# Weight buffers moved by 64 bytes, gated and summed tokens to multiples of 128 bytes

## What is computed

```python
mod = silu(c) @ w_ada + b_ada
sh1, sc1, g1, sh2, sc2, g2, sh3, sc3, g3 = split(mod, 9)
h = modulate(rms_norm(x, ffn1_norm), sh1, sc1)
x = x + 0.5 * g1 * ((silu(h @ w1) * (h @ w3)) @ w2)
h = modulate(rms_norm(x, mix_norm), sh2, sc2)
z = h @ w_in                       # 28 tiles of 128 columns
x = x + g2 * (concat(hgrn2(z), rglru(z)) @ w_out)
h = modulate(rms_norm(x, ffn2_norm), sh3, sc3)
x = x + 0.5 * g3 * ((silu(h @ w1b) * (h @ w3b)) @ w2b)
return rms_norm(x, final_norm)
```

## The kernel before

| tile | used as | before | after |
|---|---|---|---|
| `hhi`, `hlo`, `yhi`, `ylo` | tokens | 0 | 0 |
| `ghi2`, `glo2` (gated tokens) | tokens | 64 | 0 |
| `forms` (summed tokens) | tokens | 64 | 0 |
| `whi`, `wlo` (and `raw`) | weights | 0 | 64 |
| `hix`, `lox` (weight sums) | weights | 64 | 64 |
| `whi2`, `wlo2` (units 2 and 3) | weights | 64 | 0 |

## Time and profile before

### The profile page before, as it was taken

How to read it: one execution, slowest core, us unless ns; L and a number is a source line. 1 busy time by engine, 2 the same in 40 slices (tenths; PEclk the granted TensorE clock), 3 DMA queues, 4 the chain that set the end, 5 groups by cost and what they waited for, 6 DMA issues and landing times.

```text
span 1018.0 us, 18544 instructions
## 1 busy us (share of the span) xinstructions
PE 996.2 (98%) x6942; PEld 867.3 (85%) x6942; DVE 747.5 (73%) x1039; ACT 506.2 (50%) x690; POOL 227.3 (22%) x191
## 2 busy tenths in 40 slices
PE   8999999999999999999999989999999999999997
PEld 6779999999888888786677767878999999988887
DVE  6778778777787868779899995566778777683334
ACT  5545444455332134578977973465444444433221
POOL 0024453543112301100100000202444544200100
PEclk9999999999999999999999999999999999999999
DMA  9557667674788836421121202235676676552322
GB/s 353 211 171 205 167 201 182 180 211 149 254 284 288 309 103 234 154 83 62 63 84 43 83 23 81 86 119 142 167 214 185 177 213 166 186 180 89 104 83 84
DMA packets 63190, 162.21 MB, mean 159 GB/s; under 512 B 5440, under 2 KB 7760, under 8 KB 63008
## 3 DMA queue, kind: packets, MB, share of 16 engines
q1 hardware_dynamic: 44720, 110.79, 30.4%
q0 software_dynamic: 18416, 50.68, 20.3%
HBM read 159.36 MB, written 2.10 MB: 159 GB/s over the span
## 4 chain that ended last, share of the span: by engine, by line
PE 90%; DVE 4%; ACT 3%; issue 2%; DMA 1%; SPq 0%; DVEq 0%; ACTq 0%
PE psum L1889 15%; PE psum L1891 15%; PE psum L1890 15%; PE psum L1961 12%; PE psum L1963 12%; PE psum L1962 12%; PE psum L2219 1%; PE psum L2256 1%; PE psum L2262 1%; PE psum L2190 1%; PE psum L2107 1%; PE psum L2192 1%; PE psum L2191 1%; PE psum L2276 1%; DVE wlo L1107 1%
## 5 line engine op out<-in xcount | busy, mean ns | idle before, releaser
L586 ACT ACTIVATE whi<-raw 128x1024 fp32r<-128x1024 f32 x92 | 97.2, 1057 | 227.7 <-PE psum L1891 211.0
L1107 DVE TENSOR_TENSOR wlo<-raw,whi 128x1024 fp32r<-128x1024 f32 x94 | 117.7, 1253 | 120.9 <-ACT whi L586 120.6
L1891 PE MATMUL psum<-ghi,wlo 128*128 128x512 f32 (+2 forms) x384 | 143.7, 374 | 0.0
L1890 PE MATMUL psum<-glo,whi 128*128 128x512 f32 (+2 forms) x384 | 143.4, 373 | 0.0
L1889 PE MATMUL psum<-ghi,whi 128*128 128x512 f32 (+2 forms) x384 | 143.0, 373 | 0.0
L1889 PE MATMUL psum<-hhi,whi 128*128 128x512 f32 x320 | 130.8, 409 | 2.0 <-DVE wlo L1107 1.3
L1891 PE MATMUL psum<-hhi,wlo 128*128 128x512 f32 x320 | 125.0, 391 | 0.0
L1890 PE MATMUL psum<-hlo,whi 128*128 128x512 f32 x320 | 124.9, 390 | 0.0
L1961 PE MATMUL psum<-forms,whi 128*128 128x256 f32 x432 | 121.1, 280 | 0.0
L1962 PE MATMUL psum<-forms,whi 128*128 128x256 f32 x432 | 120.5, 279 | 0.0
L1963 PE MATMUL psum<-forms,wlo 128*128 128x256 f32 x432 | 120.5, 279 | 0.0
(11 more groups left out here) (270 smaller groups left out, 2349.4 us busy)
## 6 DMA issues: line engine op xcount, KB each, us to landing
raw<-wu SPq DMA_DIRECT2D x96, 512.0 KB, 3.4
ada<-wada POOLq DMA_DIRECT2D x56, 512.0 KB, 5.1
sraw_a<-ws SPq DMA_DIRECT2D x36, 512.0 KB, 6.1
raw<-ws SPq DMA_DIRECT2D x36, 512.0 KB, 6.1
sraw_b<-ws SPq DMA_DIRECT2D x36, 256.0 KB, 3.9
sraw_a<-ws POOLq DMA_DIRECT2D x18, 512.0 KB, 6.0
raw<-ws POOLq DMA_DIRECT2D x18, 512.0 KB, 5.9
early<-wada SPq DMA_DIRECT2D x16, 512.0 KB, 15.3
```

Of the source, the lines that this page charges most:

```text
L586: nc.scalar.activation(whi[:, slot, :], raw[:, slot, :], ACT.Copy).then_inc(hi_done, 1)
L1107: nc.vector.tensor_tensor(wlo[:, slot, :], raw[:, slot, :], whi[:, slot, :], ALU.subtract).then_inc(lo_done, 1)
L1890: nc.tensor.matmul(dst, a, rlo, start=False, stop=False)
L1891: return nc.tensor.matmul(dst, b, rhi, start=False, stop=stop)
```

## The change

A constant `HALF_LINE` of 64 bytes is added at three places: ahead of `raw`, `whi` and `wlo` (which moves all that follows), ahead of `hix`, and ahead of `g2`, whose address `glo2` and, by fixed distances, `h32`, `t32`, `sq0`, `whi2`, `wlo2` and `csr0` share. No instruction, wait or order is changed.

```diff
+HALF_LINE = 64
...
         hlo = sb("hlo", [P, KD, T], F32R)
+        place[0] += HALF_LINE
         raw = sb("raw", [P, 2, UNIT])
...
-        hix, off = at("hix", [P, 3, T], F32R, off)
+        hix, off = at("hix", [P, 3, T], F32R, off + HALF_LINE)
         lox, off = at("lox", [P, 3, T], F32R, off)
...
-        g2_at = off
+        g2_at = off + HALF_LINE
```

## The result

The changed kernel takes 1026.06 us in the median (1025.79 to 1027.58, 4 runs) against 1021.4 us before on the same chip: the ratio is 1.0056, with an interval of 1.0042 to 1.0070. It is slower, where 1018.7 us and faster had been forecast. The profiled execution has a span of 1024.6 us against 1018.0 before, 6.6 us more.

A forecast was written before the change was run, and what follows sets the result against it. The prediction took PE's three-fold matmuls as the bound, their pitch set by operand places modulo 128 bytes. Its terms, -12.6 + 4.1 + 3.9 + 2.0 + 0.2 = -2.4 us, gave 1018.7 us; own range 1015 to 1022, wider range 1004 to 1026.

The forecast's parts named there:

- What bounds the kernel: Whole kernel: 81% of 1018.0 us lies on six lines of three-fold matmuls, so it gains or loses nearly what they do.
- With all 84 at 113.3 ns it takes 9.52: Group stages: a group of 84 matmuls falls from 9.854 to 9.53 us with joints, 11.7 us less over 36 groups.
- T0/W64: Tokens at 0, weights at 64 modulo 128 bytes, the change's aim: 113.3 ns at 256 columns, 233.3 at 512.
- Down projections at 512 columns: Two down-projection stages: 960 matmuls rise from 229.0 to 233.3 ns, +4.1 us.
- 256-column halves: Ends of the down projections: 192 matmuls fall from 117.8 to 113.3 ns, 0.9 us less.
- Products with `hhi` and `yhi`: Other 512-column products: 588 in long stretches at +6.6 ns, +3.9 us; 468 in the mixer at +4.3 ns, +2.0 us.
- units 2 and 3 of the opening: Opening stage, weights from `whi2` and `wlo2`: 48 matmuls fall to about 226.7 ns while 48 others worsen, net nothing.
- Value units: 96 matmuls with tokens stationary and weights moving: 229.0 against 226.7 ns, +0.2 us, bounds -1.3 and +0.6.
- A: Fast rival: 512 columns at T0/W64 also save 6.7 ns, 220.0 ns; 29.3 us less, 991.8 us; chance 0.13.
- B: Middle rival: all 512-column matmuls go at 226.7 ns; 14.8 us less, 1006.3 us; chance 0.12.
- C: Slower rival: split-weight supply holds groups at 9.854 us while 512 columns pay; +9.3 us, 1030.4 us; chance 0.10.
- D: No-change rival: pitches follow tiles and their traffic, not bytes modulo 128; 1021.1 us; chance 0.05.

The follow-up runs named there:

- m1_places: TensorE alone, none of the layer: every pair of token and weight places in 64-byte steps; 226.6 to 233.3 ns at 512 columns, 113.3 to 120.0 at 256.
- m3_widths: TensorE alone: seven widths at four distances, 16 steps of 64 bytes at 256 columns, bf16 at six distances; the steps gave 113.3 or 117.8 ns.
- m2_groups: TensorE alone: a group's seven products in order for 32 sets of places; before's set 9.853 us a group, after's 9.89, best 9.520.
- k_w192_f128_x64: Kernel before with weights and gated tokens at 192 modulo 256, `forms` 128, `hix` 64; 1015.0 us, ratio 0.9946.
- k_hix192: Changed kernel with `hix`, `lox` and the gated tokens' second half 128 bytes further, `hix` at 192 modulo 256; 1026.38 us, ratio 1.0041.
- k_w_back: Changed kernel with the weights back at 128 modulo 256, all else where the change put it; 1024.18 us, ratio 1.0021.
- k_g128: Kernel before with only the gated tokens moved, to 128 modulo 256, the weights' place; 1019.11 us, ratio 0.9984.
- k_f64_x192: Kernel before with gated tokens at 128 modulo 256 like the weights, `forms` at 64, `hix` at 192; 1015.53 us, ratio 0.9938.
- k_mixer_at_192: k_w192_f128_x64 with the mixer's and output projection's tokens 64 bytes on, at 192 modulo 256 like the weights; 1013.28 us, ratio 0.9926.

## Why the prediction was wrong

*What bounds the kernel* held: 6.6 us came from the lengths of matmuls alone, and PE stayed busy in all of the group stage. The pitches read from before were read right too; every one came back on TensorE alone.

*The step that failed* is "With all 84 at 113.3 ns it takes 9.52". It took one product's pitch, `hhi` with `hix`, for the pitch of T0/W64. That product's distance is 64, modulo 256; after the change the four pairs have the distances 64 (`hhi`, `whi`), 192 (`forms`, `whi`), 64 (`forms`, `hix`) and 192 (`hhi`, `hix`). That alone doesn't decide: at both distances m1_places and m3_widths show 113.3 and 117.8 ns. What decides where the step is 64 bytes is how the pair was entered: from equal places, one step down of either operand gives the fast one, one step up the slow one (16 of 16). The kernel before follows it. From `hhi` with `whi` (both at 128) tokens step up to `forms` (192): 117.8. From `forms` with `hix` (both at 192) tokens step down to `hhi` (128): 113.3. The change made the places differ in every pair of the groups and so took away the pairs at 120.0 ns from which the fast pitch had been entered in each group. After it the steps between products are of 128 bytes. No rule was found for these, and equal places aren't a condition: m1_places, m2_groups and the first group after the change each show 113 to 114 ns without them. What the runs do show is that this set doesn't keep the fast pitch. It was lost at the next step of the tokens by 128 bytes in the first group (114.2, then 117.9 ns) and in m2_groups (113.3, then 117.8), and 117.8 stayed. Worth 13.3 us: 11.7 forecast gained, 1.6 lost.

The prediction's last sentence had said where it could break: bytes modulo 256, `forms` at 0 and `whi` at 192, 1296 matmuls at 117.8, 1024.5 us. They did stay at 117.8; the other 432 of `hhi` with `whi`, 432 of `forms` with `hix` and 864 of `hhi` with `hix` weren't at 113.3 either, but for `forms` with `hix` in the first group of each stage.

*Down projections at 512 columns*, +4.1 us forecast, were oversized: the totals of the 960 matmuls (starts less than 1 us apart) are 220.0 and 221.2 us. `ghi` with `whi` stays at distance 192 (0 and 192 after the change, 192 and 128 before) and keeps its 228.9 ns; only the products with `glo2`, at 128, are at distance 64. Two thirds at 228.9 and one at 233.3 is 230.4 ns, the pitch measured. The 256-column halves stayed at 117.8 instead of falling (0 for -0.9).

*Products with `hhi` and `yhi`*: 233.3 ns in long stretches was right, and units 2 and 3 of the opening fell to 226.7 as forecast. Their totals rose by 232.7 - 228.6 = 4.1 and 46.5 - 45.6 = 0.9 us, where 5.9 was forecast. *Value units*: 228.3 to 229.4 ns, 96 of them, +0.1 for +0.2. These matmuls' sums are +6.3 us, the stages outside the groups show +5.0: some 1.3 us went into time between other matmuls and idle time of PE, half in the opening and half in the mixer, which the prediction, counting the mixer in full, had left out. Here 1.2 + 0 + 5.0 + 0.1 - 1.3 = 5.0.

*Rivals.* A and B asked for 220 and 226.7 ns at T0/W64 and 512 columns; 233.3 came. C named the supply of split weights as a bound on the period. The stages did keep their time and 512 columns did pay, as C has it, but not for its reason: PE waited for no `wlo` there, and k_w192_f128_x64 was supplied at 9.52 us a group. D, that places do nothing, fell with m1_places. The rule cited there, the Trainium skill, "TensorE: Matmul & The Clock Gate", Part 2, of two independent read ports between which no bandwidth is taken, doesn't give the pitch for 4-byte operands: m1_places shows 226.7 against 233.3 ns with every other engine at rest, where by the rule, as the prediction used it, 16 pairs would have shown one pitch. For bf16 the measurements agree with it (215.8 ns at six distances).

*The range* ended at 1026, just short of the median. The case that came, a placement class that the trace of before doesn't hold, had been given no chance of its own: it stood in the last paragraph alone, with a number and without a weight. The pairs that the change makes could have been written down modulo 256 from the offsets; three of the four had no row.

*Settled and not.* That distance modulo 256 sets the pitch at 512 columns, and distance with what ran before that at 256, is shown with one part moved at a time. How a step of 128 bytes chooses between the two pitches is open, so a set of places has to be measured in its order of products. Why places act so isn't shown. Nor is the cause of the waits for `wlo` of 0.6 to 3 us between 115 and 138 us, which five of the eight other layer kernels' profiled executions have (k_hix192, k_w_back, k_g128, k_f64_x192, k_mixer_at_192) and those of before and after don't: in k_g128 they go back to a late DMA, with a group's places unchanged. With what follows them they add up to some 5 us, 0.5%, to one execution, so single edits were judged by pitches and stages, and only sums of several by their time.

## What to carry to other kernels

An address change must be priced by the relation of the two operands that one instruction reads, pair by pair, before and after, in the coarsest period that the trace doesn't exclude; one pair's speed isn't a property of its class. Where a pitch is bistable (two steady values at the same addresses), a stretch at the short pitch may owe it to what ran before it: removing a neighbour at the long pitch can remove the short one too. With fp32r operands, weights and tokens at equal places modulo 256 bytes for most products of 512 columns, and a set of places for 256 columns that was measured on a small loop of the real order of products, were worth 0.7% here.

## What the runs showed of the hardware

- Two fp32r operands of a matmul with a weight load before each: 226.7, 233.3, 232.0 to 233.3 and 228.9 ns at 512 columns for distances 0, 64, 128 and 192 bytes, whatever the absolute place (16 pairs, m1_places). At 384 columns 173.3 to 176.7, at 320 no difference.
- At 256 columns one pair of tiles has two steady pitches, 113.3 and 117.8 ns, kept over hundreds of matmuls (`hhi` with `whi` in k_hix192: 113.3 in the first group stage, 118 in the second; k_w192_f128_x64: 118 in the first group of the first stage, 113.3 in its other 17).
- After a wait of PE of 2.92 us in k_g128 the granted clock was 0.54 in the next 3.6 us, near its lower level (1.2 GHz), and a matmul of 256 columns took 213 ns from start to start.
- Narrow fp32r matmuls stop at 111.4 to 111.9 ns: 192 columns take what 128 take. In bf16, 128 columns take 55.8 ns.
- The Trainium skill, "SBUF — State Buffer", section "Operand start alignment", asks that an operand starts at a multiple of its element size, and says of itself that it is about legality, not speed. Every place used here meets that; the times above differ by up to 3% at 512 columns and 6% at 256 all the same.
